# Attention of two small layers reordered: two banks for transposes, gates by tanh, convolution on VectorE alone, k norms by columns, another load order

## The chip, the cores and the metric

One core of a Trainium2 chip. The metric is the device time of one execution in microseconds (us); lower is better. Engines are named as in the profile: PE is TensorE (PEld its weight loads), DVE VectorE, ACT ScalarE, POOL GpSimd, SP the queue that issues the weight loads.

## The reference

256 tokens of width 1024 pass three residual blocks. The change touches the first two (layers 0 and 1); the third (retention, dilated attention, MLP) is left as it is.

```python
# layer 0
u_val, u_gate, z_a, q, k, v, z_b = split(rmsnorm(x) @ w_in0)          # 512 wide each
h   = causal_depthwise_conv(u_val * sigmoid(u_gate), 31 taps) + b
y_a = silu(layernorm(h)) * silu(z_a)
y_b = attention(rmsnorm_heads(q), rmsnorm_heads(k), v, alibi) * silu(z_b)      # 8 heads of 64, causal
x   = x + concat(y_a, y_b) @ w_out0
# layer 1
q_c, kc, vc, ks, vs, kw, vw, g, z_c, q_d, k_d, v_d, z_d = split(rmsnorm(x) @ w_in1)
o_c = g0*attn(q_c, compressed(kc), compressed(vc)) + g1*attn(q_c, ks, vs) + g2*attn(q_c, kw, vw)
y_c = o_c * silu(z_c)                                                 # 15 compressed keys; 256 keys each
y_d = banded_attention(q_d, k_d, v_d, window 128, sinks) * silu(z_d)
x   = x + concat(y_c, y_d) @ w_out1
# then the third block: x = x + mixer(modulate(rmsnorm(x))); x = x + mlp(modulate(rmsnorm(x))); rmsnorm(x)
```

## The kernel before

Everything is float32 and stays on the chip; only weights stream in, in units of up to 1 MB (1024 x 256). Each engine has its instruction list written out by hand, and semaphores tie the lists together. Activations stand with features on partitions (`xT`, 8 tiles of 128 x 256 tokens).

`group_plan()` writes the products down as groups in the order in which PE makes them. A group fills one of three PSUM banks (`proj0` to `proj2`, in turn), and is freed by the engine that copies it out; `proj_ready` counts the groups made, `bank_free` the copies. Units are loaded into slots (`raw`, and free stretches of `arena` and `probT`) in the order of the list `LOADS`. SP waits before a load until the group that last read the slot is done (`LAST_READ`); what stands behind it in the list waits too.

Layer 0: PE projects `uv`, `ug` (conv input), `bq`, `bk`, `bv`. DVE makes 26 of the 31 taps of the convolution (L1657, two instructions for a tap and a half of the channels); the other five are matmuls with diagonal matrices that DVE made before (L1624, L787), and L1678 adds the two. Queries are normed by columns: PE sums the squares with tokens on partitions, so that 8 numbers a token are left, and the factor is applied in the scores. Keys are normed by rows: PE sums into a 128 x 512 tile, and DVE makes variance (L1419), reciprocal (L1423) and product (L1464) on all of it.

An attention unit `u` is two times two heads of one query tile (128 queries) against `n` keys: 128 for the first tile, 256 for the second, 15 for the compressed branch. `b` has 4 units, `c` 12 (three branches of 4), `d` 4. PE makes scores (L729) into the one pair of score banks; DVE scales, adds the bias (L1489) and takes the maximum (L1498, L1500); ACT makes exp (L1162); DVE normalises (L1535); PE transposes (L741, one round for each 128 keys) into the one bank `transposed`; ACT copies that out (L1180); PE mixes with v (L770) into `mixed`; DVE multiplies with the gate (L1551). `attention()` runs this with the scores two units ahead, and puts projections of later groups between a unit's two rounds of transposes (`FILL_B`, `FILL_CD`; L819 is half a projection, `ad...` L849 a product with one row). ACT applies Silu to the gates `zb`, `za`, `zc`, `zd` in between (L1108), which needs another activation table than exp: both ways a load.

The third block's weights are split in two float32r parts: ACT makes the high part (L1096), POOL the low one (L542). `passing(name)` on ACT makes as many high parts ahead as the slots allow, wherever a group is met. In the list of ACT that is inside the last part of the attention of `c` and `d`, where `rq0` and `rq1` come in, and in the output product `wo1` for `rq2`:

```python
while state["hi"] < min(len(SPLIT), most):
    ...
    act.wait_ge(raw_in[RAW_AT[n]], raw_target(n))
    nc.scalar.activation(hi_slots[HI_AT[m]][:, 0:kt * w], raw_slots[RAW_AT[n]][:, 0:kt * w], ACT.Copy)
```

After the attention: `wo0` and `wo1` (four groups each, L598), DVE adds to `xT` (L1740), ACT squares (L1144), PE sums (L683), and the norm (L1438, L1442, L1434) opens the next layer.

Of the kernel before, what the change touches and what calls it, by code (L numbers as in the profile page):

```python
# [11 lines left out]
P = 128  # L12
# [23 lines left out]
CONV_DVE = 26  # L36
# [39 lines left out]

def around(items):

    at = items.index("/") if "/" in items else len(items)
    return items[:at], items[at + 1:]  # L80


def group_plan():
# [4 lines left out]
    out += own(["bq0", "bq1", "bk0", "bk1"]) + [("conv0", []), ("conv1", [])] + own(["bv0", "bv1"])  # L88
    out += [(n, parts_of(n)) for n in fills_of(FILL_B)]
    out += own([f"wo0_{i}" for i in range(4)]) + [(n, parts_of(n)) for n in ("ad2", "ad3")]  # L90
    out += own(["kcvc", "kskw", "vsvw", "qc0", "qc1", "vdgt"])
    out += [("hidk", ["ck0", "ck1"]), ("qd0", ["qd0"]), ("hTk", []), ("hidv", ["cv0", "cv1"]), ("kc2", []), ("hTv", []),
            ("ad4", parts_of("ad4")), ("zc0", ["zc0"]), ("vc2", []), ("ad5", parts_of("ad5"))]
# [24 lines left out]
BANK_AT = {n: i for i, n in enumerate(BANKED)}  # L118
# [45 lines left out]
LOADS.remove("wo1_3")  # L164
LOADS.insert(LOADS.index("rq1") + 1, "wo1_3")


def loads_after():
# [3 lines left out]
    for u in LOADS:  # L172
        before = RAW_BEFORE[WEIGHT_AT[u]]
        if before is not None:
            most = max(most, LAST_READ[WEIGHTS[before]])
        elif u in ALONE:
            most = max(most, GROUP_AT["wr3" if u[2] == "1" else "ad7"])
        elif u in RAW_MORE:
            most = max(most, GROUP_AT["wr0"] - 1 if u == RAW_MORE[0] else GROUP_AT["wr3"])
# [73 lines left out]
Q_NORMS = ("bq0", "bq1", "qc0", "qc1", "qd0", "qd1")  # L253
Q_GAIN = dict(b="b_qnorm_g", c="c_qnorm_g", d="d_qnorm_g")
# [3 lines left out]
def mixer_kernel(nc, a, out):  # L258
    ctx = ExitStack()
    with ctx:  # L260
# [52 lines left out]
        def place(at, *shape):  # L313
# [5 lines left out]
            if len(shape) == 3:  # L319
# [19 lines left out]
        diags = [fl(prob2[:, i // 8])[:, P * (i % 8):P * (i % 8) + P] if i < 16 else probT[:, P * (i - 16):P * (i - 15)]  # L339
                 for i in range(4 * (TAPS - CONV_DVE))]  # L340

# [53 lines left out]

        def pT(u, br, r):
# [40 lines left out]
        def bank(name):  # L437
            return pp[BANK_AT[name] % NPP]

        def evacuated(name):  # L440

            m = BANK_AT[name]
            return bank_free[m % NPP], m // NPP + 1

        def free_of(name):
            return bank_free[BANK_AT[name] % NPP]
# [10 lines left out]
        def rstd_of(name):  # L457

            return q_rstd[:, dict(b=0, c=1, d=2)[name[1] if name[0] == "q" else "b"], int(name[2])]

# [17 lines left out]
        def _(sp):  # L478
            for i in range(2):
                sp.dma_start(xT[:, 4 * i:4 * i + 4], cut(a["x"], S)[:, 4 * i:4 * i + 4]).then_inc(x_in[i], 16)  # L480
            for u in LOADS:
# [15 lines left out]
                if u == "bq1":  # L497
                    sp.dma_start(alibi, a["alibi"]).then_inc(const_in, 16)
# [35 lines left out]
        def _(pool):  # L534
# [11 lines left out]
            nc.gpsimd.memset(probT[:, 0:512], 0.0).then_inc(sem("cmp_zero"), 1)  # L546
            for u in SPLIT:
# [4 lines left out]
        def _(pe):  # L552
            state = dict(filled=0, norm=0, head=0, stream=0, lo=-1)

            def begin(name):
                m = BANK_AT[name]
                assert state["filled"] <= m < state["filled"] + NPP, name
                if m >= NPP:
                    pe.wait_ge(bank_free[m % NPP], m // NPP)
                return pp[m % NPP]  # L560
# [127 lines left out]
            def head_sums(name):  # L688
# [7 lines left out]
                if name in Q_NORMS:  # L696

                    for i in range(4):
                        t, c = divmod(i, 2)
                        last = nc.tensor.matmul(st[:, 2 * i:2 * i + 2], sq[:, S * c + P * t:S * c + P * t + P],  # L700
# [4 lines left out]

            def scores(u):
                part, step, br, last_br, at, qt, n = UNITS[u]

                if part in "cd" and (u == 0 or UNITS[u - 1][0] != part or br == 0):
                    pe.wait_ge(norm_done, NORM_AT["kd" if part == "d" else "cmp" if br == 0 else "qc1"] + 1)  # L710
# [22 lines left out]
            def transposes(u, r):  # L733
# [3 lines left out]
                if rounds_before(u) + r:  # L737
                    pe.wait_ge(pt_ready, rounds_before(u) + r)
                for i in range(3 if part == "a" else 4):
                    w = min(n - P * r, P)  # L740
                    last = nc.tensor.transpose(pt[0:w, P * i:P * i + P], prob(u)[:, i, P * r:P * r + w], ident[:])  # L741
# [38 lines left out]
            def convolution(i):  # L780

                b = begin(f"conv{i}")
                for j in range(2):
                    c = 2 * i + j
                    for k in range(TAPS - CONV_DVE):
                        tap = CONV_DVE + k
                        last = nc.tensor.matmul(b[:, S * j:S * j + S], diags[4 * k + c], hpad[:, c, tap:tap + S],  # L787
                                                start=k == 0, stop=tap == TAPS - 1)
                end(last)

            def between(name):
                if name[:2] == "S:":
                    head_sums(name[2:])
# [46 lines left out]

            def ada(name, silu=silu_c):
# [1136 lines left out]
```

## Time and profile before

| | us |
|---|---|
| median of the timed runs | 1037.6 (lowest 1036.6) |
| the profiled execution's own time | 1039.65 |
| its span, first to last instruction | 1037.9 |
| PE busy | 958.2 (92%) |
| DVE, ACT, POOL busy | 394.5, 409.2, 467.6 |

The span is what the rows below share out; the time of the execution lies 1.75 us above it, and 2.05 us above the median. Idle time of an engine counts only where the next thing that ends the span waits for it.

### The profile page before, as it was taken

The page shows a single profiled execution, that of the slowest core. Times are in us where ns is not written, and L with a number is a line of the kernel's source. Part 1 is how long each engine was busy: PE and PEld are TensorE (multiplying, and loading weights), DVE is VectorE, ACT ScalarE, POOL GpSimd, SP SyncE. Part 2 cuts the span into 40 slices and gives each one's busy share as a digit, 9 for nine tenths or more (in the row PEclk, how much of TensorE's full clock was granted, in tenths as well). Part 3 has the DMA queues.
Part 4 walks back from the last instruction along what each step waited for, and adds up shares of the span by engine and source line. Part 5 has one row for each costly group of instructions (what it writes and reads, how often), then busy time and mean ns, then how long its engine had stood idle before and what let it go on. Part 6 is the DMA issues. An engine that isn't in the chain of part 4 may idle for free.

```text
span 1037.9 us, 15403 instructions
## 1 busy us (share of the span) xinstructions
PE 958.2 (92%) x6562; PEld 855.9 (82%) x6562; DVE 394.5 (38%) x739; ACT 409.2 (39%) x588; POOL 467.6 (45%) x197
## 2 busy tenths in 40 slices
PE   5999889999896577999999999999999989999996
PEld 4887677788675366798899978999999969999996
DVE  4776421320646521851011111322113477883002
ACT  2110441013565521334443345667633445452330
POOL 0000000000000300579866677766788869987780
PEclk9999899999899589899999999999999989999998
DMA  9632245958415007275544444444544925553531
GB/s 355 250 127 76 82 173 203 348 158 335 167 41 192 12 1 305 93 237 189 203 162 136 150 162 163 157 135 157 191 175 163 386 101 185 181 190 136 196 129 41
DMA packets 27612, 177.53 MB, mean 171 GB/s; under 512 B 2920, under 2 KB 5620, under 8 KB 7064
## 3 DMA queue, kind: packets, MB, share of 16 engines
q1 hardware_dynamic: 26104, 174.35, 46.6%
q10 hardware_dynamic: 1440, 2.20, 0.7%
q8 instruction: 52, 0.85, 0.3%
q14 instruction: 16, 0.13, 0.0%
HBM read 174.95 MB, written 3.43 MB: 172 GB/s over the span
## 4 chain that ended last, share of the span: by engine, by line
PE 83%; DVE 9%; DMA 4%; ACT 2%; issue 1%; SPq 0%; DVEq 0%; ACTq 0%
PE proj L598 17%; PE proj L623 14%; PE proj L626 14%; PE proj L625 14%; DMA raw<-in_weights 4%; PE proj L819 3%; PE proj L664 2%; PE proj L663 2%; PE proj L661 2%; PE proj L645 2%; PE proj L849 2%; PE transposed L741 2%; PE mixed L770 1%; PE scores L729 1%; DVE rstd L1438 1%
## 5 line engine op out<-in xcount | busy, mean ns | idle before, releaser
L542 POOL TENSOR_TENSOR w_lo<-raw,w_hi 128x1024 fp32r<-128x1024 f32 x142 | 341.3, 2426 | 271.6 <-ACT w_hi L1096 271.6
L625 PE MATMUL proj<-parts,w_lo 128*128 128x256 f32 x800 | 226.3, 283 | 0.0
L623 PE MATMUL proj<-parts,w_hi 128*128 128x256 f32 x768 | 221.2, 288 | 3.9 <-DVE parts L1612 2.3
L626 PE MATMUL proj<-parts,w_hi 128*128 128x256 f32 x768 | 217.2, 283 | 0.0
L1096 ACT ACTIVATE w_hi<-raw 128x2048 fp32r<-128x2048 f32 x71 | 135.7, 1911 | 132.2 <-DMA raw<-in_weights 56.8
L625 PEld LDWEIGHTS proj<-parts,w_lo 128*128 128x128 f32 x800 | 153.4, 192 | 0.8 <-issue 0.7
L623 PEld LDWEIGHTS proj<-parts,w_hi 128*128 128x128 f32 x768 | 147.1, 191 | 6.7 <-issue 3.0
L626 PEld LDWEIGHTS proj<-parts,w_hi 128*128 128x128 f32 x768 | 147.0, 191 | 0.0
L546 POOL MEMSET probT<- 128x512 f32 x1 | 0.5, 524 | 248.4 <-PE proj L936 248.4
L598 PE MATMUL proj<-h,raw 128*128 128x256 f32 x320 | 74.5, 395 | 3.0 <-DVE h L1442 3.0
L598 PEld LDWEIGHTS proj<-h,raw 128*128 128x128 f32 x320 | 63.3, 199 | 13.7 <-issue 4.5
L598 PE MATMUL proj<-h,arena 128*128 128x256 f32 x256 | 56.8, 381 | 1.2 <-DVE h L1442 1.1
L598 PEld LDWEIGHTS proj<-h,arena 128*128 128x128 f32 x256 | 48.2, 190 | 10.6 <-issue 3.6
L1144 ACT ACTIVATE wide<-xT 128x512 f32<-128x512 f32 (+1 forms) x24 | 13.1, 555 | 108.8 <-DVE xT L1843 58.7
L1108 ACT ACTIVATE arena<-proj 128x512 f32<-128x512 f32 x40 | 23.9, 598 | 78.0 <-PE proj L626 48.8
L598 PE MATMUL proj<-arena 128*128 128x256 f32 x224 | 50.9, 388 | 0.0
L598 PEld LDWEIGHTS proj<-arena 128*128 128x128 f32 x224 | 43.5, 195 | 6.6 <-issue 0.5
L623 PE MATMUL proj<-hid_hi,w_hi 128*128 128x256 f32 x160 | 45.1, 282 | 0.0
L626 PE MATMUL proj<-hid_lo,w_hi 128*128 128x256 f32 x160 | 44.7, 280 | 0.0
L625 PE MATMUL proj<-hid_hi,w_lo 128*128 128x256 f32 x160 | 44.6, 279 | 0.0
L661 PE MATMUL proj<-w_hi,parts 128*128 128x512 f32 x112 | 44.4, 396 | 0.0
L1860 DVE TENSOR_TENSOR hid_lo<-tmp,hid_hi 128x512 fp32r<-128x512 f32 x16 | 43.7, 2732 | 0.6
(280 smaller groups left out, 1942.2 us busy)
## 6 DMA issues: line engine op xcount, KB each, us to landing
raw<-in_weights SPq DMA_DIRECT2D x110, 1024.0 KB, 5.0
arena<-in_weights SPq DMA_DIRECT2D x39, 1024.0 KB, 6.2
probT<-in_weights SPq DMA_DIRECT2D x8, 1024.0 KB, 5.0
dil_lines<-dil_line SPq DMA_DIRECT2D x1, 2304.0 KB, 12.1
dil_bias<-dil_lines SPq DMA_DIRECT2D x1, 1536.0 KB, 9.2
xT<-in_x SPq DMA_DIRECT2D x2, 512.0 KB, 5.5
arena<-in_alibi SPq DMA_DIRECT2D x1, 1024.0 KB, 20.5
arena<-in_swa SPq DMA_DIRECT2D x1, 1024.0 KB, 7.1
```

The lines of the kernel that those rows point to most:

```text
L542: nc.gpsimd.tensor_tensor(lo_slots[RAW_AT[n]][:, at], raw_slots[RAW_AT[n]][:, at], hi_slots[HI_AT[m]][:, at].bitcast(F32), ALU.subtract).t ...
L598: last = nc.tensor.matmul(b[:, S * j:S * j + S], w[:, k, P * j:P * j + P], src[:, k, :], start=first, stop=done and (k == ks[-1] if not wa ...
L623: nc.tensor.matmul(dst, whi, h, start=first, stop=False)
L625: nc.tensor.matmul(dst, wlo, h, start=False, stop=False)
L626: last = nc.tensor.matmul(dst, whi, lo[:, k, :], start=False, stop=stop)
L645: last = nc.tensor.matmul(b[:, S * t:S * t + n], h32[:, k, P * t:P * t + P], w[:, k, 0:n], start=k == 0, stop=k == KD - 1)
L661: nc.tensor.matmul(banks[t], parts[:, 0, kk, at], whi[:, k, :], start=kk == 0, stop=False)
L663: nc.tensor.matmul(banks[t], parts[:, 0, kk, at], wlo[:, k, :], start=False, stop=False)
L819: last = nc.tensor.matmul(b[:, 2 * c:2 * c + S], w[:, k, c:c + P], h32[:, k, :], start=k == 0, stop=k == KD - 1)
L1096: nc.scalar.activation(hi_slots[HI_AT[m]][:, 0:kt * w], raw_slots[RAW_AT[n]][:, 0:kt * w], ACT.Copy) \
L1108: nc.scalar.activation(dst, b[:], fn, scale=scale).then_inc(free_of(name), 1)
L1860: V.tensor_tensor(two(hid_lo, i), r, two(hid_hi, i).bitcast(F32), ALU.subtract).then_inc(sem("hid_ready"), 1)
```

## The change

- All 31 taps run on DVE (the bias comes in with tap 0); the diagonals, the five taps' matmuls and L1678's sum go.
- `bk0`, `bk1`, `kskw` and `kd` are normed like the queries, by columns. PE then spreads the factors over rows with a matmul of the identity against a broadcast column (`spread`, groups `sp_...`), and DVE multiplies once (`keys_out`).
- `narrow_attention` takes the place of `attention` for `b`, `c` and `d`. The third projection bank serves as a second bank for transposes there, so both rounds of a unit are made at once; groups inside use two banks. `mixed_out` comes two units late, and the fills come after the mix.
- Gates: silu(z) = z (1 + tanh(z/2)) / 2. ACT makes the tanh; DVE makes (tanh + 1) z from the bank (`gate_out`); the 1/2 goes into the mixed product.
- `qd1` and `kd` are made ahead of the attention of `c`, `ad4` and `ad5` within it. First units of a part begin earlier (scores of `b` behind `bv1`, scores of `c` around `zc0`).
- High parts are made from `wo1_0` on; POOL waits for the end of `d`. `rq0` and `rq1` are loaded ahead of `wo1_0`, `rq2` ahead of `wo1_3`, and `ad8`, `ad9` behind it.

The diff at its core (of the three `narrow_attention` the first is PE's, the second ACT's, the third DVE's):

```diff
-FILL_B = [["zb0", "L:mean"], ["zb1", "L:sq", "ad0"], ["za0", "L:act"], ["za1", "ad1"]]
+FILL_B = [x.split() for x in ("zb1 ad0 L:mean E:zb0", "za0 L:sq E:zb1 E:ad0 L:centre", "za1 E:za0 L:var", "ad1 L:scale")]
 FILL_CD = [x.split() for x in (
-    "/ qd1.0", "/ qd1.1", "/ E:qd1 kd.0", "S:qd1 / E:kd zc1.0", "S:kd / zc1.1", "/ E:zc1 zd0.0", "/ zd0.1", "/ E:zd0 zd1.0",
-    "/ zd1.1", "/ E:zd1 ad6", "/ modA", "/", "/ ad7", "/", "/", "/")]
+    "N:kd E:zc0", "zc1.0 E:kd", "zc1.1", "ad4 E:zc1", "zd0.0 E:ad4", "zd0.1", "ad5 E:zd0", "zd1.0 E:ad5", "zd1.1", "ad6 E:zd1",
+    "E:ad6", "modA", "ad7 E:modA", "E:ad7", "", "")]
...
-LOADS = [u for u in WEIGHTS if u[:3] not in ("ad8", "ad9", "ad1") or u[:4] in ("ad1a", "ad1b")]
-for _before, _us in (("rq2", ("ad8a", "ad8b", "ad9a", "ad9b")), ("f1_2", ("ad10a", "ad10b", "ad11a", "ad11b"))):
-    for _n, _u in enumerate(_us):
+LOADS = [u for u in WEIGHTS if u not in ("ad8a", "ad8b", "ad9a", "ad9b", "ad10a", "ad10b", "ad11a", "ad11b")]
+for _us, _before in ((("rq0", "rq1"), "wo1_0"), (("rq2",), "wo1_3"), (("ad8a", "ad8b", "ad9a", "ad9b"), "rq3"),
+                     (("ad10a", "ad10b", "ad11a", "ad11b"), "f1_2")):
...
+        def transposed(u, r):
+            return pt if UNITS[u][0] == "a" or (rounds_before(u) + r) % 2 == 0 else pp[2]
...
+            pool.wait_ge(po_free, STEPS_TO["d"])
             for u in SPLIT:
                 low(u)
...
+            def spread(group, c, n, name):
+                pe.wait_ge(norm_done, NORM_AT[name] + 1)
+                b = begin(group)
+                for i in range(n):
+                    for t in range(TT):
+                        for f in range(2):
+                            at = 4 * t + 2 * (c + i) + f
+                            column = rstd_of(name)[:, at:at + 1].broadcast_to([P, HD])
+                            last = nc.tensor.matmul(b[HD * f:HD * f + HD, S * i + P * t:S * i + P * t + P], column, ident,
+                                                    start=True, stop=True)
+                end(last)
...
+            def narrow_attention(units, fill):
+                for i, u in enumerate(units):
+                    for r in range(key_tiles(u)):
+                        transposes(u, r)
+                    if i + 2 < len(units):
+                        scores(units[i + 2])
+                    if i and UNITS[u - 1][3]:
+                        mix(u - 1)
+                    for name in fill[i]:
+                        between(name)
+                mix(units[-1])
...
             head_sums("bk0")
-            pe.wait_ge(sem("diags_ready"), len(diags))
-            pe.wait_ge(sem("hpad_ready"), 2)
-            convolution(0)
+            plain_tokens("bv0", 256)
             head_sums("bk1")
-            convolution(1)
-            plain_tokens("bv0", 256)
+            spread("sp_bk0", 0, 2, "bk0")
             plain_tokens("bv1", 256)
-            pe.wait_ge(norm_done, NORM_AT["bk1"] + 1)
+            scores(PART["b"][0])
+            spread("sp_bk1", 0, 2, "bk1")
+            project("zb0")
+            scores(PART["b"][1])
             pe.wait_ge(*evacuated("bv1"))
-            attention(PART["b"], FILL_B)
+            pe.wait_ge(*evacuated(last_in(2, "zb0")))
+            narrow_attention(PART["b"], FILL_B)
...
-                    if max(old, LOADED_AFTER[v]) >= GROUP_AT[name]:
+                    if max(old, LOADED_AFTER[v], GROUP_AT["wo1_0"] - 1) >= GROUP_AT[name]:
                         break
...
-                    copy_out(name, dst, fn=ACT.Silu)
+                    nc.scalar.activation(dst, ready(name)[:], ACT.Tanh, scale=0.5).then_inc(sem("z_tanh"), 1)
...
+            def narrow_attention(units, fill):
+                exps(units[0])
+                for i, u in enumerate(units):
...
+                    for name in prompt(fill[i]):
+                        between(name)
+                    if i + 1 < len(units):
+                        exps(units[i + 1])
+                    transposed_out(u, range(key_tiles(u)))
+                    for name in late(fill[i]):
+                        between(name)
...
+            def keys_out(group, src, dst, gain):
+                dve.wait_ge(*evacuated(src))
+                b = ready(group)
+                V.scalar_tensor_tensor(dst, b[:, 0:dst.shape[-1]], col(gain), dst, ALU.mult, ALU.mult).then_inc(free_of(group), 1)
+            def gate_out(name):
...
+                V.scalar_tensor_tensor(t, t, 1.0, bank(name)[:], ALU.add, ALU.mult).then_inc(free_of(name), 1)
...
+            def narrow_attention(units, fill, begun=0, ending=lambda: None):
+                for u in units[0:2] if not begun else ():
+                    score_max(u)
+                for i, u in enumerate(units):
+                    if i or not begun:
+                        normalise(u)
+                    for name in prompt(fill[i]):
+                        between(name)
+                    if i >= 2 and UNITS[units[i - 2]][3]:
+                        mixed_out(units[i - 2])
+                    if i + 2 < len(units):
+                        score_max(units[i + 2])
+                    for name in late(fill[i]):
+                        between(name)
...
+            taps(0, 14, TAPS)
+            for i, name in enumerate(("bq0", "bq1")):
                 variance(name)
-                taps(1, 2 + 7 * i, min(9 + 7 * i, CONV_DVE))
...
+            variance("bk0")
+            taps(1, 14, 17)
...
+            score_max(PART["b"][0])
+            keys_out("sp_bk1", "bk1", fl(bkT[:, 2:4]), "b_knorm_g")
+            taps(1, 22, 27)
+            normalise(PART["b"][0])
+            taps(1, 27, TAPS)
...
+            score_max(PART["b"][1])
```

## Rows read from the trace of the kernel before

**Rows 1.** The page's second part: granted clock of PE, tenths, in 40 equal slices.
```profile
PEclk9999899999899589899999999999999989999998
```
**Rows 2.** Windows by stage: us; busy us (instructions) of each engine; clock; DMA.
```profile
76.04:168.21 92.17, 82.89 (x421) 65.83 (x421) 41.89 (x74) 30.72 (x64) 0.00 (x0) 0.93 0.36 129
...
196.08:267.95 71.87, 67.88 (x424) 56.43 (x425) 19.70 (x50) 19.88 (x47) 0.52 (x1) 0.99 0.77 282
267.95:331.10 63.15, 58.37 (x390) 46.01 (x390) 35.72 (x101) 38.64 (x107) 0.00 (x0) 0.95 0.23 82
331.10:376.83 45.73, 22.94 (x167) 14.62 (x167) 22.63 (x56) 20.59 (x58) 9.25 (x4) 0.70 0.15 64
376.83:406.82 29.99, 29.99 (x132) 26.16 (x133) 3.78 (x7) 1.89 (x3) 0.00 (x0) 0.95 0.41 148
406.82:421.95 15.13, 7.87 (x39) 2.40 (x38) 4.26 (x7) 4.20 (x6) 4.67 (x2) 0.77 0.61 251
421.95:1037.90 615.95, 598.34 (x4572) 570.65 (x4572) 212.27 (x309) 275.68 (x275) 452.97 (x186) 0.99 0.48 169
```
**Rows 3.** The chain of waits, 325 to 346 us: start, us, what.
```profile
327.82 11.60 DMA raw<-in_weights
...
339.45 1.91 ACT w_hi L1096
```
**Rows 4.** Timeline of attention: transposes, mix, normalising, scores, a stall [idle before].
```profile
157.30 0.66 PE L741 MATMUL transposed<-cols,prob 128*128 128x128 f32 x4
...
157.88 0.66 PE L770 MATMUL mixed<-probT,arena 128*64 128x128 f32 x8
...
284.54 1.22 DVE L1535 TENSOR_TENSOR prob<-prob,stat 128x1024 f32<-128x1024 f32 x1
...
312.52 1.14 PE L729 MATMUL scores<-arena 64*128 64x256 f32 x8
...
344.48 1.11 PE L741 MATMUL transposed<-cols,wide 128*128 128x128 f32 x4 [12.53 <-ACT probT L1180]
```
**Rows 5.** Windows of PE alone, and of all engines: us, busy, clock, DMA share, GB/s.
```profile
354.00:356.00 2.00, 2.00 (x14) 0.50 0.03 8
...
360.00:373.00 13.00, 6.83 (x74) 4.75 (x70) 8.40 (x21) 6.67 (x23) 0.00 (x0) 1.00 0.00 0
```
**Rows 6.** The chain of waits, 400 to 422 us.
```profile
401.00 12.22 DMA raw<-in_weights
...
415.73 2.09 PE sums L683 x4
```
**Rows 7.** Groups of lines, 0 to 420 us: busy, mean ns | idle before.
```profile
L787 PE MATMUL proj<-arena,prob 128*128 128x256 f32 x32 | 7.6, 379 | 0.0
...
L1108 ACT ACT_TABLE_LOAD x7 | 9.0, 1283 | 0.1
```
**Rows 8.** The chain of waits of the whole span: PE's column sums, a projection, an `ad` product.
```profile
60.44 0.79 PE sums L700 x8
61.22 7.01 PE proj L598 x32
...
133.60 1.85 PE proj L849 x16
```
**Rows 9.** Timeline around the start of attention `b` on DVE.
```profile
61.34 5.63 DVE L1657 SCALAR_TENSOR_TENSOR arena<-arena,cols 128x256 f32<-128x256 f32 x14
...
83.08 3.34 DVE L1423 RECIPROCAL rstd<-rstd 128x512 f32<-128x512 f32 x1
...
86.46 0.75 DVE L1464 SCALAR_TENSOR_TENSOR arena<-arena,cols,rstd 128x512 f32<-128x512 f32 x1
...
108.97 1.66 DVE L1489 SCALAR_TENSOR_TENSOR prob<-scores,q_rstd,arena 128x256 f32<-128x256 f32 x4 [1.39 <-PE scores L729]
...
110.74 1.22 DVE L1498 TENSOR_REDUCE stat<-prob 128x4 f32<-128x1024 f32 x1
```
**Rows 10.** Page part 5: POOL's low parts.
```profile
L542 POOL TENSOR_TENSOR w_lo<-raw,w_hi 128x1024 fp32r<-128x1024 f32 x142 | 341.3, 2426 | 271.6 <-ACT w_hi L1096 271.6
```

More of the change, by code:

```diff
@@ L35 @@
 HROW = 32
-CONV_DVE = 26
 ARENA = 18568
@@ L74, in fills_of, with late, prompt @@
     return list(dict.fromkeys(x.split(".")[0] for items in fill for x in items if x != "/" and x[1] != ":"))
+def late(items):
+    return [x for x in items if x[:2] == "L:"]
+def prompt(items):
+    return [x[2:] for x in items if x[:2] == "E:"]
 def around(items):
@@ L117, with take_banks, last_in @@
 BANKED = [g for g in GROUPS if f"{g}:1" not in GROUP_AT]
-BANK_AT = {n: i for i, n in enumerate(BANKED)}
+FILL_AT = {n: i for i, n in enumerate(BANKED)}
+TWO = {"zb0", "zc0", "sp_kd", *fills_of(FILL_B), *fills_of(FILL_CD)}
+def take_banks():
+    bank, uses, last, count = {}, {}, {}, {}
+    for n, g in enumerate(BANKED):
+        b = min(range(2 if g in TWO else NPP), key=lambda x: last.get(x, -1))
+        bank[g], uses[g] = b, count.get(b, 0)
+        last[b], count[b] = n, uses[g] + 1
+    return bank, uses
+BANK_OF, USES = take_banks()
+def last_in(b, group):
+    return [g for g in BANKED[:FILL_AT[group]] if BANK_OF[g] == b][-1]
 SPLIT = [u for u in WEIGHTS[WEIGHT_AT["rq0"]:] if u[:2] != "ad"]
@@ L176, in loads_after @@
         elif u in ALONE:
-            most = max(most, GROUP_AT["wr3" if u[2] == "1" else "ad7"])
+            most = max(most, GROUP_AT["wr3" if u[2] == "1" else "wo1_0"])
         elif u in RAW_MORE:
@@ L778, in token_sums @@
                 last.then_inc(sem(done), 1)
[L780 to L789, printed above, removed]
             def between(name):
-                if name[:2] == "S:":
-                    head_sums(name[2:])
+                if name == "N:kd":
+                    spread("sp_kd", 0, 1, "kd")
                 elif name[:2] == "ad":
@@ L960, in _ @@
             hidden_columns(1, "hTv", "hidv")
-            ada("ad4")
-            project("zc0")
+            project("qd1")
             head_sums("cmp")
+            project("kd")
+            head_sums("qd1")
             pe.wait_ge(*evacuated("hTv"))
@@ L970, in _ @@
             end(last)
-            ada("ad5")
+            scores(PART["c"][0])
+            chunk("zc0", "0")
+            head_sums("kd")
+            scores(PART["c"][1])
+            chunk("zc0", "1")
             pe.wait_ge(*evacuated("vsvw"))
@@ L1329, in _ @@
             root("cmp")
-            between("zc0")
+            head_squares("kd", kdT)
+            root("qd1")
+            root("kd")
             table(ACT.Exp)
-            attention(PART["c"] + PART["d"], FILL_CD)
+            narrow_attention(PART["c"] + PART["d"], FILL_CD)
             table(ACT.Sqrt)
@@ L1605, in attention @@
                 mixed_out(units[-1])
+            every = lambda ap: ap.unsqueeze(1).broadcast_to([P, 4, S])
+            y_a = yT0[:, 0:4]
+            def narrow_attention(units, fill, begun=0, ending=lambda: None):
[12 more added lines that the diff above has]
+                        between(name)
+                if UNITS[units[-2]][3]:
+                    mixed_out(units[-2])
+                ending()
+                mixed_out(units[-1])
             def operand_low(pieces):
@@ L1619, in _ @@
             dve.wait_ge(first_in, 16)
-            def diagonals(lo, hi):
-                for i in range(lo, hi):
-                    k, c = divmod(i, 4)
-                    V.tensor_scalar(diags[i], ident, conv_col(c, CONV_DVE + k), None, ALU.mult).then_inc(sem("diags_ready"), 1)
             for i in range(2):
@@ L1653, in taps @@
                         if tap == 0:
-                            own.did(V.tensor_scalar(y, h, conv_col(c, 0), None, ALU.mult))
+                            own.did(V.tensor_scalar(y, h, conv_col(c, 0), col("a_conv_b", c), ALU.mult, ALU.add))
                         else:
```

236 lines of the change are left out of this document (124 added, 112 removed).

## The prediction, made before the change ran

> **What bounds the kernel now.** I read the windows by stage first, the granted clock next, and the chain of waits where PE idles. PE is the bound: from 421.95 us to the end it is busy 598.34 of 615.95 us [rows 2], and nothing there is edited but the numbering of banks. What can be won lies in 76.04 to 421.95 us. There PE loses time in three ways. It waits for the softmax: 92.17 - 82.89 = 9.3 us in 76.04 to 168.21, and 4.0, 4.8 and 22.8 us in the three windows from 196.08 to 376.83 [rows 2]. It waits 12.53 us in one piece before a transpose at 344.48 [rows 4]: the chain there is a weight load of 11.60 us, then ACT's high part of 1.91 us [rows 3]. That load belongs to the third block; ACT stands before it with the next exponentials behind. The same happens in the output product: a load issued at 401.00 lands 12.22 us later, and PE's sums start at 415.73 [rows 6]. Third, after each such gap the granted clock is 0.50, PE's lower level of 1.2 GHz: while PE was busy all of 354 to 356 us [rows 5], and in the slices with a 5 or an 8 [rows 1].
>
> **The change, term by term.** The sum goes against the profiled execution, 1039.65 us (span 1037.9), 2.05 us above the median of 1037.6.
>
> Term 1, from the end of bk1's projection (76.04) to the end of wo0_0 (168.21). Of 92.17 us I take off PE's idle 9.3; the five taps' matmuls, 40 records of which the larger group has 32 [rows 7], at a pitch of 7.01 / 32 = 0.22 us [rows 8], 8.8; and the low clock: a grant of 0.93 over 92.17 us is 6.5 us short [rows 2], some 5.5 of it in busy time. That leaves 68.6 us of work. Added are two spreads of eight products with 64-wide stationary operands; no row shows one. Nearest is the mix, 0.66 us for four [rows 4], so 1.3 each at most by that row; four column sums took 0.79 [rows 8], so 1.6 by that. I take 1.1, the mix without its start, 2.2 in all: 70.8. Below nothing it cannot go, as the work is new.
>
> What is late next is DVE. It has 62 instructions for the taps of channels 2 and 3 from 61 us on, at 5.63 / 14 = 0.40 us [rows 9], 24.9 us, and the ten added for channels 0 and 1 before them (4.0) now fill a gap in front of the query sums. It loses the two key reciprocals of 3.34 us [rows 9] for ones of 8 columns. Laid out, DVE ends the taps near 104 us and the first scaling of the second unit (1.66 us [rows 9]) near 105.4. PE reaches the third scores at 102.7, and must wait for that scaling since there is one pair of score banks: 3 us. Everything of PE (zb1, ad0, the mean) is queued behind that wait. After it PE has about 44.4 us without another wait of note: the layer norm's chain on DVE and ACT (centre, sqrt, scale, Silu, both products) comes to its end near 144 to 145 us, when PE has just done the two chunks of wo0_0 that the new order puts in front. The 3 us gap should bring the lower clock, as the first 8 among the slices, at 104 to 130 us, does behind such gaps [rows 1]; I charge 3 us (0 to 6). So 70.8 + 3 + 3 = 76.8, and term 1 is -15.4 (-10 to -19).
>
> Term 2, layer 1 until the end of its attention (196.08 to 376.83, 180.75 us). Up to the first transposes the window of 71.87 us [rows 2] gains qd1 and kd (7.01 and half of it [rows 8]), their sums and two spreads (2.8), and loses ad4 and ad5 (1.85 each [rows 8]) and 3.6 of the 4.0 us of waits: 77.9. Then 16 units. In one step PE makes the transposes of u and the scores of u+2 (T), and then the mix and the fill (F); DVE meanwhile scales and takes the maximum of u+2 and normalises u+1 (S), and can't begin before PE's scores. So a step is T plus the larger of F and S, plus 0.25 us of handing over. With 0.62 us a round of transposes (0.66 with its start [rows 4]), 0.6 to 1.14 a set of scores [rows 4], 3.5 half a projection, 1.85 an ad product [rows 8], 0.6 to 2.4 a mix, and on DVE 1.66 + 1.22 for 256 keys [rows 9], about two thirds of that for 128, 1.25 for the 15, and 1.22 plus 0.4 of small instructions for normalising 256 keys [rows 4], T sums to 25.8 us, the larger ones to 59.2 (F alone 40.5) and handing over to 4: 89 us. S wins in nine steps of the 16; the last six cost 32 us, as the fills have run out. Gates and mixed products on DVE fall into T, when DVE waits anyway. That costs nothing as long as T is longer; a gate (0.75 us, by the key product [rows 9]) and a mixed product, 0.45, stay under the 1.25 us of the shortest T with a gate in its step. Without this cover they add 12 us.
>
> Before, the part from 267.95 was 63.15 + 45.73 = 108.9 us; the stall of 12.5 and its low clock go, since ACT no longer makes high parts there. All high parts fall behind `wo1_0`'s start: three of 1.91 [rows 3] against some 11 us until the first square is due, and six low parts of 2.43 [rows 10] against the 30 us of the output product. POOL's new wait holds only those, and the first to need one is rq0's product. 77.9 + 89 = 166.9; I add 5 us for the low clock in the thin last steps (0 to 10): 171.9, so -9 (-3 to -14). For the charge speaks that 331 to 377 us ran at 0.70 [rows 2]; against a larger one, that 360 to 373 us, with PE busy 6.83 of 13 us, ran at 1.00 [rows 5].
>
> Tanh has no row; I take it at Silu's time, and without the table loads of 1.283 us that stood at the Silu gates [rows 7]. By the Trainium skill (ScalarE: Activation LUTs, table sets) tanh is in the set of exp, and a switch of sets costs 2.66 us by its figure. The trace has 1.283 for a load [rows 7], and the measured one stands.
>
> Term 3, output product to the start of rq0. 29.99 us stay, the slow start with them [rows 2]. In 15.13 us, rq2's load no longer comes behind ad8 and ad9, and ACT's squares don't wait for it. Without that, wo1_3's sum and square end near 408.2, but ad8 holds PE until 409.3; from the sums on 421.95 - 415.73 = 6.2 us follow, 1.0 less with the sums at full clock [rows 6]. rq0 starts at 414.5: -7.5 (-7 to -9). SP passes rq0 and rq1 before wo1_0; they wait for ad5, read well before zd1, which wo1_0 waits for, so nothing is held up. rq2 waits for ad7, three steps from the end. Behind it stand wo1_3 (due 14 us after its slot comes free) and ad8 and ad9, as late as before.
>
> The diagonals cost nothing and give nothing: DVE waited there. Sum: -15.4 - 9.0 - 7.5 = -31.9; 1039.65 - 31.9 - 2.05 = 1005.7, and I say **1005 us**.
>
> **The rivals.** A: DVE becomes the bound in layer 1. Gates, ad columns and mixed products (12 us) don't fit under T, and term 2 is gone: 1005 + 10 = 1015. For it: PE's part of a step is often the shorter. Against: DVE was busy 35.72 of 63.15 us [rows 2].
>
> B: the change doesn't do what it says, because tanh needs a table of its own. Then six gates among the exponentials cost two loads each, 15 us of ACT, about half of it hidden, since ACT has some 3.5 us of work in a step of 5.5: 1012. The Trainium skill (same page and section) says otherwise; no run here shows it.
>
> C: the loads still come late in the output product, because DMA takes ad9 and rq3 together. Term 3 falls away: 1013.
>
> D, slower: small gaps in every step bring the lower clock and keep it. At half, PE's 66.3 us of layer 1's steps become 133, so F exceeds S in most and the stage lasts about 137 in place of 94, +43; in layer 0 the 44.4 us after the gap double, less the 3 charged, +41. 1005 + 84 = 1089. It decides from some 33 us of busy PE at half clock beyond my charge, where the gain is gone. For it: 0.50 under a busy PE [rows 5]. Against: 1.00 at half load in 360 to 373 us [rows 5]. The Trainium skill (TensorE: Matmul & The Clock Gate, a second HAM failure mode) tells of micro-idles between groups of matmuls that make the clock swing. By that rule D is what this kernel would do; the second row speaks against it.
>
> **Chances and range.** Forecast 0.60, A 0.18, B 0.08, C 0.09, D 0.05. The measurement tells about 2% from no change: faster is below 1016.8. Terms at their good ends give 1037.6 - 42 = 995.6, at their bad ends 1037.6 - 20 = 1017.6. A to C lie inside. Below the good end lie a quarter of the 22.7 us of waits that I left in the steps (89 - 66.3), and at the other end two rivals together reach 1022; I give 990 to 1021. Faster 0.86, same 0.10 (bad ends, or A with B), slower 0.04 (most of D).
>
> **What would show it.** Right: no high part on ACT before wo1; no table load at a gate; one PE wait of about 3 us for DVE at the third scores of `b`, wo0_0 ending near 152 us; a step of layer 1 near 5.5 us with DVE or PE waiting 1 to 3 us; sums of x2 within 4 us of wo1_3; from rq0 on 616 us. Wrong: a granted clock of 0.5 through the steps, a load ending PE's waits, DVE without idle in layer 1, or a third block that takes another time than before.

## The result, and the profile after

The changed kernel takes 998.4 us (median; 997.7 to 998.7), the one before 1037.1 beside it: a ratio of 0.963 with a 95% interval of 0.961 to 0.965. One of the four executions of the kernel before took 1234.86 us and does not enter the ratio. Run again as a control (below) it gave 0.962 (0.961 to 0.964).

| | us |
|---|---|
| median of the timed runs | 998.4 |
| the profiled execution's own time | 998.33 |
| its span | 996.5 |
| PE busy | 942.4 (95%) |
| DVE, ACT, POOL busy | 389.4, 388.8, 467.5 |

The windows by stage, cut where [rows 2] are cut: from bk1's end, from wo0_0's end, from kcvc (layer 1's first projection), the first transposes of layer 1, step 11 of its 16, the output product, its end, and from rq0 (the third block's first product) to the end. Columns as in [rows 2].

```profile
77.11:150.46 73.35, 70.21 (x426) 57.05 (x425) 41.05 (x88) 25.57 (x61) 0.00 (x0) 1.00 0.45 162
150.46:178.51 28.05, 26.94 (x139) 20.73 (x138) 6.42 (x10) 2.99 (x5) 0.00 (x0) 1.00 0.65 226
178.51:256.70 78.19, 77.04 (x467) 66.57 (x467) 15.31 (x50) 19.50 (x48) 0.52 (x1) 1.00 0.64 226
256.70:311.40 54.70, 50.50 (x373) 37.02 (x373) 35.34 (x98) 25.86 (x101) 0.00 (x0) 0.94 0.43 155
311.40:344.08 32.68, 20.50 (x179) 14.73 (x175) 21.51 (x62) 14.70 (x52) 0.00 (x0) 0.79 0.27 98
344.08:373.40 29.32, 29.32 (x139) 25.30 (x142) 6.17 (x8) 7.34 (x6) 14.12 (x6) 1.00 0.45 162
373.40:380.47 7.07, 4.77 (x37) 1.47 (x37) 3.87 (x7) 2.40 (x5) 0.00 (x0) 1.00 0.83 343
380.47:996.50 616.03, 599.02 (x4572) 573.06 (x4572) 213.14 (x309) 275.88 (x275) 452.63 (x186) 0.99 0.47 169
```

Three stages are shorter than in [rows 2]: 73.35 us for 92.17, 78.19 + 87.38 = 165.57 for 180.75, and 29.32 + 7.07 = 36.39 for 45.12. That is -18.8, -15.2 and -8.7 us; the third block has its 616 us again. POOL no longer works inside the attention: its first low part runs in the output product.

The timeline of PE shows every wait of the attentions longer than 0.1 us, but the one of 0.74 ahead of the first transposes of layer 1, and the wait for x2's norm (the idle time before, and what ended it, in brackets).

```profile
107.00 0.71 PE L795 MATMUL scores<-arena 64*128 64x128 f32 x8 [2.75 <-DVE prob L1591]
...
260.53 1.12 PE L809 MATMUL proj<-cols,wide 128*128 128x128 f32 x4 [2.07 <-DVE wide L1637]
...
274.50 0.66 PE L809 MATMUL proj<-cols,prob 128*128 128x128 f32 x4 [0.98 <-DVE prob L1637]
...
300.17 0.61 PE L809 MATMUL transposed<-cols,prob 128*15 128x128 f32 x4 [0.18 <-DVE prob L1637]
...
306.47 0.66 PE L809 MATMUL proj<-cols,prob 128*128 128x128 f32 x4 [0.98 <-DVE prob L1637]
...
316.47 0.61 PE L809 MATMUL proj<-cols,prob 128*15 128x128 f32 x4 [3.37 <-DVE prob L1637]
...
323.78 1.11 PE L809 MATMUL transposed<-cols,prob 128*128 128x128 f32 x4 [4.08 <-DVE prob L1637]
...
337.61 1.12 PE L809 MATMUL proj<-cols,prob 128*128 128x128 f32 x4 [4.11 <-DVE prob L1637]
...
342.99 1.09 PE L838 MATMUL mixed<-probT,arena 128*64 128x128 f32 x16 [0.62 <-DVE arena L1653]
...
380.47 0.35 PE L669 MATMUL proj<-parts,w_hi 128*128 128x256 f32 x1 [2.30 <-DVE parts L1533]
```

Where one piece of 12.53 us stood before a transpose in [rows 4], there are now six of 1 to 4 us in layer 1, each ended by DVE's normalising (L1637), none by a load. The granted clock around three of them, in windows of 2 us:

```profile
104.00:106.00 2.00, 0.25 (x3) 0.01 (x1) 1.97 (x7) 0.00 (x0) 0.00 (x0) 1.00 0.77 311
106.00:108.00 2.00, 0.99 (x10) 0.88 (x11) 1.90 (x4) 0.00 (x0) 0.00 (x0) 1.00 0.38 160
...
324.00:326.00 2.00, 2.00 (x14) 1.45 (x13) 0.52 (x3) 0.92 (x5) 0.00 (x0) 0.50 0.00 0
...
382.00:384.00 2.00, 2.00 (x11) 2.00 (x11) 2.00 (x6) 1.15 (x4) 0.00 (x0) 0.50 0.00 0
```

In this execution the wait at 107.00 left it at 1.00 (in others it did not, see e6); after those at 316 and 323.78, and after the one ahead of rq0, it is 0.50 (1.2 GHz) while PE is busy all the time.

### The profile page after: what moved, and what is told of

Same layout as the page of the kernel before. It is cut to its first block, busy times and chain, and to the rows that moved or that the text cites. A ratio compares the mean times of both kernels' runs of the same rounds, so it can differ in the third digit from the quotient of the medians.

```text
span 996.5 us, 15476 instructions
## 1 busy us (share of the span) xinstructions
PE 942.4 (95%) x6598; PEld 849.8 (85%) x6598; DVE 389.4 (39%) x743; ACT 388.8 (39%) x574; POOL 467.5 (47%) x197
## 4 chain that ended last, share of the span: by engine, by line
PE 87%; DVE 7%; DMA 2%; ACT 2%; issue 1%; DVEq 0%; ACTq 0%
PE proj L644 18%; PE proj L669 15%; PE proj L672 15%; PE proj L671 15%; PE proj L707 3%; PE proj L710 3%; PE proj L709 3%; PE proj L691 2%; PE scores L795 2%; PE proj L876 2%; PE proj L920 1%; DMA raw<-in_weights 1%; PE mixed L838 1%; PE transposed L809 1%; DVE rstd L1537 1%
## 5 line engine op out<-in xcount | busy, mean ns | idle before, releaser
L669 PEld LDWEIGHTS proj<-parts,w_hi 128*128 128x128 f32 x768 | 148.6, 194 | 7.8 <-issue 3.9
L672 PEld LDWEIGHTS proj<-parts,w_hi 128*128 128x128 f32 x768 | 148.6, 193 | 0.0
L644 PE MATMUL proj<-h,raw 128*128 128x256 f32 x368 | 84.1, 389 | 3.2 <-DVE h L1541 3.0
L644 PEld LDWEIGHTS proj<-h,raw 128*128 128x128 f32 x368 | 70.9, 195 | 14.4 <-issue 4.2
L644 PE MATMUL proj<-h,arena 128*128 128x256 f32 x224 | 49.6, 381 | 1.1 <-DVE h L1541 1.1
L644 PEld LDWEIGHTS proj<-h,arena 128*128 128x128 f32 x224 | 42.2, 190 | 8.8 <-issue 2.4
L1803 DVE SCALAR_TENSOR_TENSOR arena<-arena,cols 128x256 f32<-128x256 f32 x120 | 48.2, 475 | 0.0
L1188 ACT ACTIVATE arena<-proj 128x512 f32<-128x512 f32 x34 | 20.3, 598 | 70.7 <-PE proj L672 48.8
```

The lines of the kernel that those rows point to most:

```text
L644: last = nc.tensor.matmul(b[:, S * j:S * j + S], w[:, k, P * j:P * j + P], src[:, k, :], start=first, stop=done and (k == ks[-1] if not wa ...
L669: nc.tensor.matmul(dst, whi, h, start=first, stop=False)
L672: last = nc.tensor.matmul(dst, whi, lo[:, k, :], start=False, stop=stop)
L1188: nc.scalar.activation(dst, b[:], fn, scale=scale).then_inc(free_of(name), 1)
L1803: own.did(V.scalar_tensor_tensor(y, h, conv_col(c, tap), y, ALU.mult, ALU.add))
```

## The experiments

The kernel before took 1038.7, 1039.1 and 1037.9 us beside the three groups of four runs. At the control's ratio the changed kernel would be at 999.4 and 999.8 us in the first two; in the third it was run (998.7).

**Which part gave what: the rule on high parts alone, and all but it.** `e1_gate_alone` is the kernel before with the new `LOADS` and

```diff
-                    if max(old, LOADED_AFTER[v]) >= GROUP_AT[name]:
+                    if max(old, LOADED_AFTER[v], GROUP_AT["wo1_0"] - 1) >= GROUP_AT[name]:
...
+            pool.wait_ge(po_free, STEPS_TO["d"])
             for u in SPLIT:
```

> The kernel before with nothing but the new load order and the rule that high parts start with wo1_0. My theory: the stall of 12.5 us in attention goes, with it some 4 us of low clock behind it, and 7.5 us in the output product: 1037 - 24 = 1013 us, so most of the gain, with the order of attention worth the other 15. Rival: the stall only gives way to DVE's chain, which then ends last in the same steps: 1037 - 7.5 - 6 = 1023 us, and the new order of attention is what makes room.

`e2_gate_undone` takes the same lines out of the changed kernel, with the old `LOADS`.

> The changed kernel with the old load order and without the rule on high parts and POOL's wait: they are made in attention again. My theory: ACT waits for rq0's load ahead of the next exponentials as before, 12.5 us and some low clock, and the output product loses 7.5 to 8: 998 + 24 = 1022 us. Rival: in the new order ACT meets the loads at steps where they have landed, and only the output product is longer: 1006 us.

Measured: 1019.4 us, 0.981 (0.980 to 0.983), and 1016.8 us, 0.978 (0.975 to 0.980). Both lie between theory and rival. The two halves of the change are worth about the same, some 19 and 22 us, and nearly add up (41 of 39). By stage, windows of e1 (layer 0 from bk1's end, layer 1 to the end of attention, output product, rest):

```profile
77.24:194.77 117.53, 107.14 (x559) 84.94 (x558) 48.31 (x84) 33.72 (x69) 0.00 (x0) 0.97 0.44 155
194.77:363.26 168.49, 147.33 (x981) 115.82 (x981) 74.34 (x205) 75.79 (x210) 0.53 (x1) 0.93 0.48 174
363.26:400.37 37.11, 34.81 (x172) 27.52 (x171) 8.20 (x14) 9.33 (x11) 14.12 (x6) 0.98 0.50 194
```

and of e2:

```profile
76.28:179.38 103.10, 98.85 (x564) 78.97 (x562) 47.46 (x98) 28.57 (x66) 0.00 (x0) 0.98 0.50 177
179.38:356.65 177.27, 150.47 (x1013) 120.33 (x1013) 75.73 (x209) 63.58 (x200) 10.24 (x5) 0.90 0.43 159
356.65:401.03 44.38, 38.13 (x172) 28.64 (x171) 8.03 (x14) 6.09 (x9) 4.66 (x2) 0.89 0.48 185
```

Below, "the rule" stands for all that e1 has: the rule on high parts, POOL's wait and the load order; no run parts these three. Layer 1 up to the output product takes 180.75 us before, 168.49 with the rule alone, 177.27 with the rest of the change alone, and 165.57 with both. The rule gives 12 us, with either order; all the rest gives 3. The output product takes 45.12, 37.11, 44.38 and 36.39, so nearly all of its gain is the rule's. Layer 0 from bk1's end takes 120.04 (76.04 to 196.08 in [rows 2]), 117.53, 103.10 and 101.40: there the rest gives 16 to 17 us. The 2.5 and 1.7 us left between the kernels with the same order I don't put down to the rule: PE's waits agree to 0.01 us, and what differs is busy time at a low clock. No run takes the gain in layer 0 apart, so what the taps, the column norms and the order of `b` give there is read from busy and idle time only.

My 24 us for the rule were 5 too many. Of the 12.5 + 4 us for the stall and its clock, layer 1 shows 12.3: 10.4 of idle time (31.6 to 21.2) and 1.9 of busy time (149.2 to 147.3). The clock is still 0.93 there, as PE still waits for DVE in the last steps; in that the rival was right (timeline).

```profile
353.47 0.66 PE L743 MATMUL transposed<-cols,prob 128*128 128x128 f32 x4 [2.19 <-DVE prob L1537]
...
357.39 1.12 PE L743 MATMUL transposed<-cols,prob 128*128 128x128 f32 x4 [2.06 <-DVE prob L1537]
```

In e2 the stall is back, longer than the wait that DVE alone sets there (4.08 above); timeline, and the chain of waits:

```profile
333.21 1.11 PE L807 MATMUL transposed<-cols,prob 128*128 128x128 f32 x4 [12.62 <-DVE prob L1635]
```
```profile
314.05 12.04 DMA raw<-in_weights
...
326.12 0.08 ACT w_hi L1174
...
380.86 11.45 DMA raw<-in_weights
...
392.33 0.02 ACT w_hi L1174
```

The wait is put down to DVE, but the chain shows that it goes back to a load of 12.04 us on which ACT's high part waits, with the exponentials behind it; the second load does the same to the squares of x2.

**The tables.** `e3_silu_gates`:

```diff
-                    nc.scalar.activation(dst, ready(name)[:], ACT.Tanh, scale=0.5).then_inc(sem("z_tanh"), 1)
+                    nc.scalar.activation(dst, ready(name)[:], ACT.Silu).then_inc(sem("z_tanh"), 1)
```

> The changed kernel with Silu in place of tanh in ACT's eight gates (so the gates hold other values; the work is the same but for the table loads). Two loads of 1.283 us at a gate: some 14 more loads, 18 us of ACT. My theory: tanh is in exp's table, and without that about half of the loads stand on the path: 998 + 7 = 1005 us (1002 to 1010). Rival: ACT has room in each step and hides all of them: 998 to 1000 us.

Measured: 999.5 us, 0.962 (0.961 to 0.964), no different from the changed kernel. The groups of ACT by line, 77 to 345 us, of e3 (gates, exponentials) and below it of the changed kernel (gates):

```profile
L1274 ACT ACT_TABLE_LOAD x8 | 10.3, 1283 | 0.1
L1246 ACT ACT_TABLE_LOAD x7 | 9.0, 1283 | 0.1
```
```profile
L1274 ACT ACT_TABLE_LOAD x1 | 1.3, 1283 | 0.0
```

Gates and exponentials have 15 loads where the changed kernel has one; the layer norm's Silu behind za1 needs none of its own now, so that there are 13 more in all, 16.7 us of ACT. One wait of PE grows (2.91 us for the 2.07 at 260.53); in the time nothing can be measured, so ACT hides them, as the rival had it. That tanh shares exp's table, as the Trainium skill (ScalarE: Activation LUTs, table sets) has it, is borne out: of the eight gates only za1's, which stands behind a Sqrt, has a load.

**The second bank.** `e4_one_bank`:

```diff
-            return pt if UNITS[u][0] == "a" or (rounds_before(u) + r) % 2 == 0 else pp[2]
+            return pt
...
-                    for r in range(key_tiles(u)):
-                        transposes(u, r)
+                    transposes(u, 0)
                     if i + 2 < len(units):
                         scores(units[i + 2])
                     if i and UNITS[u - 1][3]:
                         mix(u - 1)
+                    if key_tiles(u) == 2:
+                        transposes(u, 1)
```

> The changed kernel with one bank for transposes; the second round of a unit comes behind the scores and the mix and waits for ACT's copy of the first. Theory: PE's part of a step ahead of the scores lies on the path, so eight units with two rounds lose 0.6 to 1 us each: 1004 to 1006 us. Rival: the scores and the mix cover the copy, and the second bank is worth nothing: 998 to 1000 us.

Measured: 1004.6 us, 0.967 (0.965 to 0.968): in the new order the second bank is worth some 5 us, and layer 1's steps take 92.45 us for 87.38 (window below, 258.98 to 351.43). The number came out, the mechanism for the smaller part. Three second rounds of layer 1 wait 0.75 us for ACT's copy of the first, as in the timeline's row, but other waits shrink, and PE's idle time in the steps grows by 1.2 us only (17.55 for 16.38). The other 3.9 us are busy time, at a clock of 0.85 for 0.88. Nor is this what the second bank gave over the kernel before: there one bank served as well, but with a projection between a unit's two rounds, which e4 doesn't have.

```profile
280.58 0.66 PE L809 MATMUL transposed<-cols,prob 128*128 128x128 f32 x4 [0.76 <-ACT probT L1265]
```
```profile
258.98:351.43 92.45, 74.90 (x547) 53.49 (x547) 56.54 (x160) 41.56 (x152) 0.00 (x0) 0.85 0.36 126
```

**The clock in layer 1's attention.** `e5_idle_filled` and `e10_idle_matched` put products that nobody reads behind the fills; e10's counts are {0: 5, 2: 2, 8: 2, 10: 7, 11: 9, 13: 9}.

```diff
+IDLE = {0: 8, 2: 3, 8: 3, 10: 13, 11: 15, 13: 15}
...
+            def idle(n):
+                for i in range(n):
+                    nc.tensor.matmul(st[:, 0:S], ident, xT[:, i % KD, :], start=True, stop=True)
...
                     for name in fill[i]:
                         between(name)
+                    if UNITS[units[0]][0] == "c":
+                        idle(IDLE.get(i, 0))
```

> The changed kernel with products that nobody reads (128x256, 0.22 us each: 8, 3, 3, 13, 15 and 15 of them) where PE waits in steps 1, 3, 9, 11, 12 and 14 of layer 1's attention. Theory: the granted clock of 0.50 in 259 to 265, 317 to 327 and 338 to 341 us follows PE's idle time, and costs 2.5 + 2.0 + 1.6 = 6 us; filled, the clock stays at 1.00: 992 to 994 us. Rival 1: DVE sets these steps and what PE loses at half clock is hidden: 997 to 999 us. Rival 2: the products come in the way of the transposes: over 1000 us.

e5 measured 999.6 us, 0.962 (0.961 to 0.964), with the clock at 1.00 through the attention. I had misread the price: a product is two records, 0.44 us. Its timeline has 5.88 us of them in the wait of 3.37:

```profile
312.23 5.88 PE L901 MATMUL sums<-xT,cols 128*128 128x256 f32 x26
```

So the full clock and the delay cancelled (its steps take 89.4 us at 1.00), and the run told nothing of the clock's worth. e10 was run with the control:

> The changed kernel as it is, as the measure for the three runs beside it: a ratio of 0.963 to the kernel before, and its gap of 2.75 us again without a fall of the granted clock.

> The run with filled idle time again, with as many products as fit: one took 0.44 us there and not 0.22, so now 5, 2, 2, 7, 9 and 9 of them. Theory: the clock stays at 1.00 and nothing comes late, so the 6 us that half clock cost come back: 5 us under the control (993 to 995 if that is 998.4). Rival: DVE sets these steps, the clock is worth nothing there, and the time is the control's within 1.5 us.

The control: 998.7 us. e10: 994.6 us, 0.958 (0.956 to 0.960), 4 us less. The attention's window in e10, against 87.38 us at 0.88 in the changed kernel (256.70 to 344.08):

```profile
257.64:340.20 82.56, 79.62 (x614) 59.50 (x614) 56.74 (x160) 40.26 (x151) 0.00 (x0) 1.00 0.40 141
```

The steps take 4.8 us less with more work on PE, and nothing else was edited: PE's idle time is what lowers the clock here, and the price of that is 4.8 us.

**The clock in layer 0.** `e6_longer_gap`:

```diff
-            taps(1, 17, 20)
             keys_out("sp_bk0", "bk0", fl(bkT[:, 0:2]), "b_knorm_g")
             variance("bk1")
-            taps(1, 20, 22)
...
-            taps(1, 22, 27)
+            taps(1, 17, 27)
             normalise(PART["b"][0])
```

> The changed kernel with ten of DVE's tap instructions (five taps) that stood ahead of the first unit's scores moved behind them, so that the scaling of the second unit comes 4.0 us later. Theory: PE's wait at the third scores grows from 2.75 to 6.9 us, and this longer gap brings the granted clock of 0.50 for some us behind it: 998.4 + 4 + 3 = 1005.5 us. Rival 1: the clock stays at 1.00 behind a gap of 6.9 us as well: 1002.5 us. Rival 2: DVE's idle time of 5.2 us ahead of the first scores takes the place, and the taps' order doesn't matter: 998 us.

Measured: 1004.0 us, 0.966 (0.965 to 0.968), 4 us more. PE's waits there are now 2.36 and 4.31 us, 3.9 more in all, and behind them the clock does fall (windows of 2 us):

```profile
106.00:108.00 2.00, 0.19 (x2) 0.00 (x0) 2.00 (x6) 0.00 (x0) 0.00 (x0) 0.95 0.08 33
108.00:110.00 2.00, 0.00 (x0) 0.00 (x0) 1.97 (x7) 0.00 (x0) 0.00 (x0) 0.50 0.00 0
...
112.00:114.00 2.00, 2.00 (x6) 1.55 (x6) 1.90 (x6) 2.00 (x9) 0.00 (x0) 0.50 0.00 0
114.00:116.00 2.00, 2.00 (x9) 1.74 (x8) 1.41 (x3) 0.26 (x1) 0.00 (x0) 0.84 0.00 0
...
76.65:183.97 107.32, 99.16 (x563) 79.25 (x562) 47.60 (x98) 28.57 (x66) 0.00 (x0) 0.97 0.48 169
```

Layer 0 takes 107.32 us from bk1's end, for 101.40 (73.35 + 28.05): 5.9 more, of which the waits are 3.9 and the clock 2.0. My guess of 3 for the clock was somewhat high.

But the run doesn't show that the longer wait is what brings the low clock. Eight profiles have the wait of 2.75 us unedited. In three of them (the changed kernel, its control, e5) the clock stays at 1.00 behind it; in the other five (e2, e3, e4, e8, e10) it falls to 0.50, and the product behind the scores, zb1, takes 8.86 us for 7.17. The timeline has zb1 of the changed kernel (its wait is shown above), and below it the wait and zb1 of e8:

```profile
107.65 7.17 PE L644 MATMUL proj<-h,arena 128*128 128x256 f32 x32
```
```profile
106.41 0.71 PE L795 MATMUL scores<-arena 64*128 64x128 f32 x8 [2.75 <-DVE prob L1590]
107.05 8.86 PE L644 MATMUL proj<-h,arena 128*128 128x256 f32 x32
```

So the low clock behind this wait comes in some executions and not in others, for 1.7 us when it comes, hardly less than the 2.0 behind e6's longer waits.

**The wait itself, and a better order.** `e7_zb1_first`:

```diff
+                    early = fill[i][0:1] if fill[i][0:1] == ["zb1"] else []
+                    for name in early:
+                        between(name)
                     if i + 2 < len(units):
                         scores(units[i + 2])
...
-                    for name in fill[i]:
+                    for name in fill[i][len(early):]:
                         between(name)
```

> The changed kernel with zb1's product ahead of the third scores of b on PE. Theory: the wait of 2.75 us goes and nothing else becomes late, as the step is longer than DVE's part of it: 995.6 us. Rival 1: the layer norm's chain then ends last at wo0_0 (a wait of 0.39 us there grows to 3.1): 998.4 us. Rival 2: scaling of the third unit becomes late for the next step: 998 to 1000 us.

Measured: 995.6 us, 0.958 (0.957 to 0.960): the wait of 2.75 us goes, the wait at wo0_0 stays at 0.39, and neither rival shows. Against the 999.8 us of its group that is 4.2 us, more than the wait; the low clock that follows it in some executions may be the rest, which is not shown. `e8_halves_early`:

```diff
-    "E:ad6", "modA", "ad7 E:modA", "E:ad7", "", "")]
+    "E:ad6", "modA", "ad7 E:modA", "E:ad7 H:0", "", "H:1")]
...
-TWO = {"zb0", "zc0", "sp_kd", *fills_of(FILL_B), *fills_of(FILL_CD)}
+TWO = {"zb0", "zc0", "sp_kd", "wo1_0", "wo1_1", *fills_of(FILL_B), *fills_of(FILL_CD)}
...
+                elif name[:2] == "H:":
+                    output_half(f"wo1_{name[2]}", 0, yT1, y_of(1))
...
-                if i == 0:
-                    for j in range(2):
-                        output_half(f"wo1_{j}", 0, yT1, y_of(1))
```

> The changed kernel with the first halves of wo1_0 and wo1_1 (3.5 us each, they need the compressed branch's heads alone) put into steps 14 and 16 of layer 1's attention. Theory: PE's wait of 4.1 us in step 14 and 0.6 in step 16 is filled, and the clock behind it stays up (1.6 us): 998.4 - 5.5 = 993 us (992 to 995). Rival: wo1_0's weights or a bank come late, or DVE's part of the step grows by as much: 998 us.

Measured: 993.8 us, 0.957 (0.955 to 0.958), 6 us less. `e11_three_steps` joins both with a third step, on DVE:

```diff
+                small = lambda i: 0 < i < len(units) and UNITS[units[i]][6] == NCMP
                 for i, u in enumerate(units):
-                    if i or not begun:
+                    if (i or not begun) and not small(i):
                         normalise(u)
...
                         mixed_out(units[i - 2])
+                    if small(i + 1):
+                        normalise(units[i + 1])
                     if i + 2 < len(units):
                         score_max(units[i + 2])
```

> Three steps on the changed kernel: zb1 ahead of the third scores; the halves of wo1_0 and wo1_1 in steps 14 and 16; and DVE normalises the compressed units (15 keys) ahead of the next scaling instead of behind it. Theory: 2.75, 5.5 and some 3 us (PE's wait of 3.4 us in step 11 goes, the next step begins earlier by as much): 11 us under the control, 987 us. Rival: the third step only moves the wait to step 12, where DVE still has all its work: 8 us under the control, 990 us.

`e12_three_steps_filled` adds `idle` to it, with {0: 5, 2: 2, 8: 2, 11: 9}, and four such products into `pt` ahead of rq0.

> The same, with products that nobody reads where PE still waits (steps 1, 3, 9 and 12, and four ahead of rq0). Theory: the clock stays at 1.00 through the attention and at rq0's start, worth 3 to 5 us more: 983 us. Rival: no gain, or some us lost, because the waits have moved and the products come in the way: 987 to 990 us.

Measured: 987.5 us, 0.952 (0.950 to 0.954), and 983.0 us, 0.947 (0.945 to 0.949), the fastest; both beat the kernel before and the changed one. In e11 the wait of 3.37 us became two of 0.58 and 0.52, and the next one is 4.68 for 4.08, so that 0.6 us are handed on. From the transposes of step 11 to those of step 13, PE takes 16.71 us (307.13 to 323.84) where e8 takes 19.41 (312.96 to 332.37): the step gives 2.7 us, near the 3 expected, 1.7 of them as waits and the rest as busy time at a higher clock.

```profile
309.45 0.61 PE L809 MATMUL proj<-cols,prob 128*15 128x128 f32 x4 [0.58 <-DVE prob L1639]
310.58 1.13 PE L795 MATMUL scores<-arena 64*128 64x256 f32 x8 [0.52 <-DVE prob L1593]
...
316.76 1.11 PE L809 MATMUL transposed<-cols,prob 128*128 128x128 f32 x4 [4.68 <-DVE prob L1639]
```

e12's first 360 us without the start, in one window, have the clock at 1.00 and 6.4 us of idle PE:

```profile
14.90:360.00 345.10, 338.71 (x2039) 276.15 (x2040) 166.73 (x423) 103.99 (x285) 14.80 (x7) 1.00 0.55 194
```

## Why the prediction was right, and where its terms were off

The direction, the three places and their order of size came out. The sum was too careful: it forecast -31.9 us for the profiled execution, and the span fell by 41.4. The term most off is the length of layer 1's steps.

**Term 1** (-15.4 forecast, -18.8 measured). Work of 70.8 us was forecast, and PE is busy 70.21; a spread, for which there was no row, takes 1.09 us for the 1.1 assumed (timeline, at 85.63). For the wait at the third scores 3 us were forecast, and it is 2.75, for the scaling that was named. For the low clock 3 us were charged, and this execution has none. That is luck: behind the same wait five of the other seven profiles have it, for 1.7 us. So the charge was mis-sized, nearly twice too large where the low clock comes. I took it from the first 8 of the slices in [rows 1], as if any gap of 3 us had it. Chance stands on the other side too: e1, with the old order and the same waits, is 2.5 us shorter in layer 0 than the profiled execution of before. wo0_0 ended at 150.46, forecast "near 152".

**Term 2** (-9 forecast, -15.2 measured). Up to the first transposes 77.9 us were forecast, and they are 78.19; for the low clock 5, and it is 4.8 by e10. The steps were forecast at 89 us, and take 82.6 at full clock (e10). The forecast left PE 22.7 us of waits in them, with DVE ending last in nine steps; the timeline has 16.4 in eight places, one of them 0.18 us and one ahead of the last mix instead of transposes. That is the step that was off, by 6 us: the chain of scaling, maximum and normalising on DVE was named rightly, but taken too long, by 4.4 us in the first ten steps (52.6 in e10 for 57) and by 2.0 in the last six (30.0 for 32). The term also hid its parts: a stall of 12.5 that goes, against -9 in all, means that I let the new order cost 3 us; e1 and e2 show it giving 3.

**Term 3** (-7.5 forecast, -8.7 measured). The part behind wo1 takes 7.07 us for the forecast 7.6, and wo1 itself 29.32 for 29.99, at a clock of 1.00 for 0.95. The sums begin at 375.19, 2 us after wo1_3.

**The rest.** From rq0 on it is 616.03 for 615.95, as forecast. Two things stood outside the terms. bk1 ended 1.1 us later, because the first 128 records on PE took 30.31 us for 29.40; the other runs with the same start had 29.37 to 30.65, so it is not the change. And the 2.05 us by which the profiled execution of before lay above its median, which I took off at the end, do not appear in the profile after, which lies at its median. Against the forecast the terms are -3.4, -6.2 and -1.2, and +1.4 lies outside them: 9.4 us too careful for the profiled execution. Taking off the 2.05 hid some of it by luck: against 1005.7 the median is 7.3 lower.

**The rivals.** A (DVE the bound): DVE is busy 56.85 of the 87.38 us of the steps, so it isn't. But PE's waits there all end with DVE's chain, and no run takes the gates off DVE, so whether they lengthen it is open. B (tanh's table): no; and e3 shows that it would have cost nothing near the 7 us that I gave it. "No table load at a gate" failed for za1. C (loads late in wo1): no; no load ends a wait of PE there, and e2, with the old load order, shows what that costs (44.38 us). D (low clock kept): the granted clock is 0.94 and 0.79 in the steps and 1.00 ahead of them. The swings of the rule on micro-idles (the Trainium skill, TensorE: Matmul & The Clock Gate, a second HAM failure mode) are there, but cost 4.8 us in the steps and not 84 in all.

## What to carry to other kernels

A change of many parts deserves a table of two by two: here two lines on when ACT and POOL may touch the next block's weights, with a load order to match, give half of the gain, and the attention order rewritten for layer 1 3 us of it. An engine that waits for a load with others' work queued behind it shows up under another engine's name; follow the chain to the load. Look at one wait in several profiles before charging it with a low clock: one execution shows one outcome. Where the bound engine must idle for some us, move real work there first (e8), and try work that nobody reads for what is left (e10, e12).

## What was not expected of the hardware

- Useless products made the kernel faster, by 4 us (e10) and 4.6 (e12 against e11), and nothing else was edited: the clock of the steps went from 0.88 to 1.00 in e10.
- One and the same wait lowers the clock in some executions and not in others. 2.75 us in layer 0 was followed by 0.50 in five profiles of eight (under e6). 2.30 us ahead of rq0 was followed by it in four of eleven: the changed kernel (0.50 at 382 us), its control, e6 and e10; e1, e3, e4, e5, e7, e8 and e11 have 1.00 there (e7's row stands below; its wait ends at 380.45). What decides was not settled.

```profile
382.00:384.00 2.00, 2.00 (x18) 1.96 (x17) 2.00 (x6) 1.15 (x4) 0.00 (x0) 1.00 0.00 0
```

- Thirteen more table loads of 1.283 us in layers 0 and 1 (e3) left nothing in the time that can be told from noise: 0.962 with them (0.961 to 0.964) and 0.962 without (the control, 0.961 to 0.964).
